# Padded value weights filled by quarters of a tile's tokens, a second projection half kept through a layer, and thirteen row slots instead of fourteen

## What is computed

```
h = rmsnorm(x); proj = h @ w_in            # q, k, v, output gate, pool input, 8 gate columns
mix = concat(mLSTM heads, pooling group) @ w_out;  x = x + mix
q = rmsnorm(x) @ peer_wq                   # 8 heads x 2 halves of 128
top 16 of 128 keys per half, 16 best of the 256 sums -> 16 experts per head, 128 per token
x = x + sum over the 128 experts of gate * gelu(xn . u_tab[e]) * v_tab[e]
x = x + sigmoid(x @ w_gate) * (p[l] @ w_ple)
```

## Time and profile before

| | |
|---|---|
| median of 3 runs | 1910.49 us (1908.98 to 1910.65) |
| the profiled execution | 1893.48 us, its span 1891.7 us |
| TensorE, VectorE, ScalarE, GpSimd busy | 1079.0, 978.1, 192.3, 998.2 us |
| bytes moved | 685.11 MB, mean 362 GB/s |
| of these gathered rows | 553.72 MB in 1056 gathers |
| of these weight halves | 103 loads into `wring`, 2 into `kept`, 1 into `scratch`, 1 MB each |

### The profile page before, as it was taken

How to read it: one execution, slowest core, us unless ns; L and a number is a source line. 1 busy time by engine, 2 the same in 40 slices (tenths; PEclk the granted TensorE clock), 3 DMA queues, 4 the chain that set the end, 5 groups by cost and what they waited for, 6 DMA issues and landing times. The chain is left out here.

```text
span 1891.7 us, 17959 instructions
## 1 busy us (share of the span) xinstructions
PE 1079.0 (57%) x6318; PEld 499.7 (26%) x6318; DVE 978.1 (52%) x2585; ACT 192.3 (10%) x332; POOL 998.2 (53%) x1062
## 2 busy tenths in 40 slices
PE   8840257788955835385655874048885522045556
PEld 4420133433412422241112432024341211031113
DVE  1498975523445788954004576951344497850001
ACT  3200021201101200000000212000110000000002
POOL 0156534345465555656666353755446566656663
PEclk9965668789987967697676886578896765576678
DMA  8699869889999999989999799979999999999995
GB/s 333 244 359 379 337 244 410 337 359 399 357 360 406 423 410 421 404 343 419 371 366 386 256 421 365 408 286 418 368 337 366 402 374 381 396 330 372 368 367 206
DMA packets 172759, 685.11 MB, mean 362 GB/s; under 512 B 19616, under 2 KB 21344, under 8 KB 158190
## 3 DMA queue, kind: packets, MB, share of 16 engines
q0 software_dynamic: 152064, 553.72, 75.9%
q1 hardware_dynamic: 20606, 130.25, 17.3%
HBM read 677.66 MB, written 6.59 MB: 362 GB/s over the span
## 5 line engine op out<-in xcount | busy, mean ns | idle before, releaser
L2105 DVE SCALAR_TENSOR_TENSOR rows<-rows,acc 128x1024 f32<-128x1024 f32 x512 | 594.2, 1217 | 49.6 <-issue 26.7
L908 PE MATMUL bank<-wring,turned 128*128 128x512 f32 (+1 forms) x808 | 394.0, 635 | 40.6 <-DMA wring<-in_w 24.3
L1235 PE MATMUL acc<-rows,wz 128*32 128x512 f32 x1952 | 323.1, 783 | 143.6 <-DMA rows<-in_v,index_tb 102.6
L1450 POOL DMA_INDIRECT rows<-in_u,index_A x256 | 240.3, 939 | 303.2 <-DVE rows L2105 123.8
L1450 POOL DMA_INDIRECT rows<-in_v,index_ta x256 | 242.5, 947 | 234.1 <-PE acc L1235 142.2
L1450 POOL DMA_INDIRECT rows<-in_u,index_B x256 | 240.7, 940 | 179.1 <-DVE rows L2105 110.7
L1450 POOL DMA_INDIRECT rows<-in_v,index_tb x256 | 241.1, 942 | 138.7 <-issue 68.1
L908 PEld LDWEIGHTS bank<-wring,turned 128*128 128x128 f32 x808 | 160.5, 207 | 236.7 <-issue 205.7
L1235 PEld LDWEIGHTS acc<-rows,wz 128*32 128x32 f32 x1952 | 69.6, 130 | 351.9 <-issue 347.0
L1185 PE MATMUL bank<-xn_s,consts 128*128 128x128 f32 x256 | 48.6, 334 | 154.3 <-issue 154.3
L1185 PEld LDWEIGHTS bank<-xn_s,consts 128*128 128x128 f32 x256 | 42.9, 243 | 159.9 <-issue 159.9
(11 more groups left out here) (320 smaller groups left out, 1054.4 us busy)
## 6 DMA issues: line engine op xcount, KB each, us to landing
wring<-in_w SPq DMA_DIRECT2D x103, 1024.0 KB
out_sample<-scratch SPq DMA_DIRECT2D x2, 2128.5 KB
scratch<-in_c_s SPq DMA_DIRECT2D x2, 2064.0 KB
rows<-in_u,index_A POOLq DMA_INDIRECT x256
rows<-in_v,index_ta POOLq DMA_INDIRECT x256
rows<-in_u,index_B POOLq DMA_INDIRECT x256
rows<-in_v,index_tb POOLq DMA_INDIRECT x256
kept<-in_w SPq DMA_DIRECT2D x2, 1024.0 KB
```

The costliest lines, as they stand in the source:

```text
L908: ins = pe.matmul(ps[:, part], turned["A"][:, 4 * h + c, :], w[:, c, part], start=first, stop=end, skip_group_check=True)
L1235: ins = pe.matmul(acc[i * QUAD:(i + 1) * QUAD, c, :], wz[:, i, at:at + QUAD], row, start=first, stop=end, skip_group_check=True)
L1450: pool.indirect_dma_start(out=rows[:, n % RING, :], out_offset=None, in_=a[table], in_offset=bass.IndirectOffsetOnAxis(ap=which[:, at:at + ...
L2105: dve.scalar_tensor_tensor(u, u, 1.0, acc[:, :, :], ALU.mult, ALU.mult, accum_out=dots[kind][:, s:s + 1]).then_inc(u_used, 1)
```

## The change

`TURN` becomes 8: `wz` holds the weights of 8 tokens of each quad, `w_later` those of the other 24, and there is a refill in front of groups 8, 16 and 24 of each big tile. `KEPT` = 2 halves of the input projection are kept through a layer: the first halves of blocks 0 and 1, each with semaphores of its own. `RING` becomes 13. In bytes of a partition: `wz` 8704 to 4608, `w_later` 256 to 384, `rows` 57344 to 53248, `kept` 8192 to 16384.

```diff
-RING = 14
+RING = 13
-TURN = QUAD // 2
+TURN = QUAD // 4
+KEPT = 2
 def is_kept(e):
-    return e[0] == "project" and e[2:4] == (0, 0)
+    return e[0] == "project" and e[2] < KEPT and e[3] == 0
@@ groups_of
-            if KIND[t] != "S" and g == TURN:
-                out.append(("refill", t))
+            if KIND[t] != "S" and g and g % TURN == 0:
+                out.append(("refill", t, g // TURN))
@@ build
-        kept = sb("kept", P, 4, BLOCK)
+        kept = sb("kept", P, KEPT, 4, BLOCK)
-        wz = sb("wz", P, 4, TURN * (QUAD + 1) + TURN)
-        w_later = sb("w_later", P, 4, TURN)
+        wz = sb("wz", P, 4, TURN * (QUAD + 1) + QUAD - TURN)
+        w_later = sb("w_later", P, 4, QUAD - TURN)
-            return (QUAD + 1) * (g % TURN) + TURN - lane
+            return (QUAD + 1) * (g % TURN) + QUAD - TURN - lane
@@ TensorE
-                    pe.wait_ge(kept_in, 16 * (layer_of(PASS_TILES[e[1]][0]) + 1))
-                    return kept
+                    pe.wait_ge(kept_in[e[2]], 16 * (layer_of(PASS_TILES[e[1]][0]) + 1))
+                    return kept[:, e[2]]
-                        ins.then_inc(kept_used, 1)
+                        ins.then_inc(kept_used[j], 1)
-                if kind != "S" and g == TURN:
-                    pe.wait_ge(refilled, count(("refill",), ("refill", t)))
+                if kind != "S" and g and g % TURN == 0:
+                    pe.wait_ge(refilled, count(("refill",), ("refill", t, g // TURN)))
@@ SyncE
-            def load_kept(layer):
-                sp.dma_start(kept[:, :, :].rearrange("p c n -> p (c n)"), a["w"][layer, IN0]).then_inc(kept_in, 16)
-
-            load_kept(0)
+            def load_kept(layer, j):
+                sp.dma_start(kept[:, j].rearrange("p c n -> p (c n)"), a["w"][layer, IN0 + 2 * j]).then_inc(kept_in[j], 16)
+
+            for j in range(KEPT):
+                load_kept(0, j)
             for e in HALVES_IN_ORDER[0:WRING]:
                 load_half(e)
                 if e == HALVES_IN_ORDER[1]:
                     load_small()
-                    sp.wait_ge(kept_used, 2)
-                    load_kept(1)
+                    sp.wait_ge(kept_used[e[2]], 2)
+                    load_kept(1, e[2])
@@ VectorE
-                halves = ps[:, 0:P].rearrange("p (j n r) -> p j n r", j=4, n=2)
-                dve.tensor_copy(by_token(), halves[:, :, 0, :])
-                free(dve.tensor_copy(w_later[:, :, :], halves[:, :, 1, :]), "turn_w", t)
-
-            def refill(t):
-
-                dve.wait_ge(v_used, V_BY[PLACE["v", t, TURN * GROUP - 1]] // GROUP)
-                after(dve.tensor_copy(by_token(), w_later[:, :, :]), refilled)
+                turned_w = ps[:, 0:P].rearrange("p (j r) -> p j r", j=4)
+                dve.tensor_copy(by_token(), turned_w[:, :, 0:TURN])
+                free(dve.tensor_copy(w_later[:, :, :], turned_w[:, :, TURN:]), "turn_w", t)
+
+            def refill(t, n):
+
+                dve.wait_ge(v_used, V_BY[PLACE["v", t, n * TURN * GROUP - 1]] // GROUP)
+                after(dve.tensor_copy(by_token(), w_later[:, :, (n - 1) * TURN:n * TURN]), refilled)
```

More of the change, by code:

```diff
@@ L791, in build @@
         bank_free = [sem(f"bank_free{i}") for i in range(BANKS)]
-        kept_in, kept_used = sem("kept_in"), sem("kept_used")
+        kept_in, kept_used = [sem("kept_in_%d" % j) for j in range(KEPT)], [sem("kept_used_%d" % j) for j in range(KEPT)]
         half_used, u_used, v_used = sem("half_used"), sem("u_used"), sem("v_used")
@@ L2124, in by_token @@
             def by_token():
-                placed = wz[:, :, TURN:].rearrange("p j (r c) -> p j r c", c=QUAD + 1)[:, :, :, 0:1]
+                placed = wz[:, :, QUAD - TURN:].rearrange("p j (r c) -> p j r c", c=QUAD + 1)[:, :, :, 0:1]
                 return placed.rearrange("p j r o -> p j (r o)")
```

## The result

The changed kernel takes 1938.15 us (median of 4 runs, 1935.82 to 1941.39); the kernel before took 1909.74 us beside it (4 runs, 1902.11 to 1910.65). The ratio is 1.0152 [1.0108, 1.0196]: 28.4 us slower, where the prediction had 14.3 and a range up to 1934. The direction and the largest mechanism were right; the size was not.

What follows compares the result with a forecast made beforehand. A stream of gathers feeds the kernel, held in turn by TensorE, DMA, VectorE and GpSimd's issue. Terms 2.4 - 2.2 - 2.5 + 3 + 13.6 = +14.3 us gave 1924.8 us, range 1905 to 1934.

Steps and rivals of the forecast that it cites:

- Thirteen slots: One row less ahead after consumer hold-ups costs one gather issue in gather-bound stretches: +3 us, bounds 0 to 6.2.
- five phases that end in a gather-bound stretch: Dots and values of tile 1, dots of tiles 3 and 4, values of tile 4: 0 to 1.24 us each.
- the next term: The refills' term, said to cover the values of tiles 0 and 3: +13.6 us.
- The start: Second kept half loads ahead of small loads, so gate matmuls wait for `m_s`: +2.4 us, bounds 0 to 3.0.
- The refills: Before group 24 of tiles 0 and 3, TensorE waits for VectorE's copy behind `choose`: +6.6 and +7.0, together +13.6 us.
- The second kept half: Fewer loads: -2.5 us for passes 2 and 3 together, -2.2 us in pass 1.
- The ring wait near 297 us: TensorE's 2.2 us wait in pass 1 for a half of block 2 vanishes, as it loads earlier: -2.2 us.
- The sum: Whole kernel: all terms together +14.3 us, 1924.8 us as a median, 0.75% slower.
- Rival A: Planner puts group 23 and its refill before the first `best`, the 13.6 us fall away: 1911 us; chance 0.22.
- rival B: Only one of tiles 0 and 3 is hit, or both by half: +7.7 us, 1918; chance 0.20.
- rival C: DMA traffic is the real bound, slot costs nothing, refills come early: -4.8 us, 1905.7; chance 0.20.

Runs made afterwards that it cites:

- f4: Kernel before with thirteen slots on the chip, planner still counting fourteen, so order of work unchanged: 1743.83 us beside 1734.01, 1.0061.
- h2: Repeat of thirteen slots with the kernel before's own schedule, timed against the kernel before: 0.70% slower.
- f1: The changed kernel run again, unaltered, against the kernel before: 1752.36 us beside 1734.01, 1.0107.
- h1: The changed kernel repeated beside its parts, against the kernel before: 1.0117.
- k1: The changed kernel repeated beside its version with one kept half, against the kernel before: 1.0101.
- e4: Changed kernel with groups 23 and 24 and the refill between them moved ahead of both `best` in tiles 0 and 3: 1761.72 us, 1.016 against the kernel before.
- e3: Changed kernel with SyncE's first loads in order of need, small loads before the second ring half: 1747.52 us, 1.0068 against the kernel before.
- after: The changed kernel with the whole change, first timed against the kernel before: 1938.15 us for 1909.74, 1.0152.
- e2: Kernel before with quarters and three refills only, one kept half and fourteen slots: 1744.18 us, 1.0057.
- g3: Quarters, one kept half and a fifteenth slot, against the kernel before: 1919.82 us beside 1908.27, 1.0053.
- g4: Quarters, one kept half, fifteen slots, last refill between the two `best`, group 25 ahead of `soften`: 1925.34 us beside the kernel before's 1908.27, 1.0077.
- g1: Changed kernel with one kept half (`KEPT = 1`), against the kernel before: 1950.34 us beside 1908.27, 1.0206.
- h4: Changed kernel with one kept half, repeated on the faster kind of chip, against the kernel before: 1.0115.
- k2: Changed kernel with one kept half, repeated beside the changed kernel, against the kernel before: 1.0114.
- the first comparison: The changed kernel's first timing beside the kernel before, 4 runs each: 1938.15 us for 1909.74, 1.0152.
- f3: Changed kernel with first loads in order of need and the refill before group 24 between the two `best`: 1744.78 us beside the kernel before's 1734.01, 1.0071.
- f2: The kernel before, unchanged, 8 runs for a profile beside the others on the same chip: 0.9993.
- h3: Repeat of quarters and three refills alone, fourteen slots, one kept half, against the kernel before: 0.91% slower.

## Why the prediction was wrong, point by point

**Thirteen slots: the failed step.** The prediction said "I count five phases that end in a gather-bound stretch [...] half: +3 us". Measured with an unchanged order of work: 0.61% and 0.70%, 9.8 and 12.4 us, above even its upper bound of 6.2. Two things were wrong in it. First, it left stretches out. The dots of tile 0 weren't counted, and the values of tiles 0 and 3 were said to be "in the next term", which then priced only the refill there. By VectorE's dots in f4 and h2 these stretches cost 4.4 and 4.6 us, nearly all in tile 0. Second, the five phases that it did count, with the sample tiles between them, cost 5.1 and 5.3 us and not 3, and the dots of tile 3 alone 2.0, where 1.24 was the most for a phase. Group 10 of tile 0 shows how a slot is lost: TensorE alternates between bursts of other matmuls and groups, and the slots are what it catches up with after each burst. There one slot less cost 1.92 us.

**The start: right place, too small.** The wait for `m_s` is 2.64 us (2.14 in f1, 1.85 in h1, 2.49 in k1, 1.27 in e4) where 2.4 was forecast. Missed was what TensorE does after it: 5.38 to 6.72 us for the first ring half in these five instead of some 3.6, at a granted clock of 0.50 in h1's slice of 18 to 22 us, the lower of the two levels, after an idle of 1.85 us. Before and in e3, without the wait, the clock stays at 1.00. The first gather went out at 90.67 to 91.60 us in the five profiles that have both kept halves in front (after, f1, h1, k1, e4; mean 91.2), at 85.47 to 88.04 in the twelve with one (mean 86.8), and at 84.85 to 88.03 in the three with e3's order (mean 86.0). So the start costs 4.4 us, 2.0 more than forecast. Where the first kept half lands moves too, between 7.5 and 10.2 us, but in kernels of either kind, so it isn't the change.

**The refills: right.** Order, place and waiting gather came as derived, and the size nearly so. Forecast 13.6 us; alone they cost 0.57% and 0.91%, 10.3 and 16.4 us, and the gathers of e2 lose 8.0 and 8.6 us at the two places. In after, where GpSimd comes late to them anyhow, each stall is 6.8 to 7.2 us instead of 9.3, and the gathers lose 5.2 to 5.3 and 5.9 to 6.0 us there (f1, h1, k1). On the faster kind of chip the other six refills added cost nothing that the runs can tell from these; g3 and g4 leave it open for the slower kind.

**The second kept half: its gain fits the forecast, but is spent by its own start.** Forecast -4.7 us beside the start. On the faster kind of chip after and after with one kept half are level: 1.0117 and 1.0115, 1.0101 and 1.0114, a mean of 0.05% or 1 us in favour of two, with intervals of 0.2% (3.5 us) on each. With 4.4 us lost at the start, it brings some 5 us elsewhere, give or take as much as the intervals. The ring wait near 297 us, which was to vanish, is gone in after; g1, with one kept half, still has 1.21 us of it at 301.96. On the faster kind of chip it isn't there with one kept half either (h4, k2), so that part of the term can't be told there.

**The sum.** On the faster kind of chip: 4.4 (start) + 11 (slot) + 13 (refills) - 5 (kept half) = 23 us. Measured were 18.4, 20.9 and 15.5. The parts aren't quite additive, since a gather that is late already waits less at the next stall: the refills' two places cost 11.2 us by the gathers in after and 16.6 in e2. With the slot at 11 and the start at 4.4 the prediction's own sum would have been +24.3 us.

**What stays open.** In the first comparison the loss was 28.4 us, on a chip where the kernel before takes 1910 and not 1733 us; and there after stood at 1.0152 while the same kernel with one kept half stood at 1.0206 (g1, in another set of runs). This suggests that on such a chip a kept half is worth more (0.5%, some 10 us, net of its start). The two never ran side by side there, and their intervals overlap, so it is not shown. Nor was the slot, the start or the refills timed alone on such a chip, so the 4 us between 24.3 and 28.4 are unexplained. Rival A (refills early) and rival B (one tile only) are excluded by the profile of after, and rival C (faster) by the time. A's price was wrong too: in e4 and f3 a refill placed earlier moves the wait on.

No version tried beats the kernel before. The best form of the whole change has e3's start, at 1.0068.

## What to carry to other kernels

Price a buffer slot over every stretch, also those that another term of the sum deals with, and over every place where its consumer works in bursts; a run with one slot less and the order of work unchanged measures it in one go. A copy of 0.2 us on an in-order engine costs what stands in front of it on that engine, and moving it up only pays if the one that it waits for is done by then: ask at each candidate place which wait comes next. And keep resident loads behind what the first matmuls need, since a short wait of TensorE can be paid twice, by the wait and by the slower clock after it.

## What the runs showed of the hardware

The same program took 1733 us on some chips and 1909 on others. One difference shows in GpSimd's gathers. With 16 of them in a pure value stretch, the fast kind needs 19.9 us, 1.24 each, the slow kind 22.8: there GpSimd stands for some 3.3 us once in 16 gathers, and no engine of the kernel ends that idle time. The kernel before on the first chip, GpSimd in that stretch, and its row in the waits of the whole span:

```profile
920.75 0.94 POOL L1450 DMA_INDIRECT rows<-in_v,index_tb  x1 [3.25 <-remote]
```
```profile
POOL rows L1450 <- remote: 51.2, 25, 3.3
```

After has 59.5 us of this in 35 waits on that chip; f1 and f2 have none. What causes it wasn't tried. The 51.2 us are less than a third of the 176 us between the two kinds. A second difference is TensorE's longest wait for a weight half: 18.61 us in the kernel before on the first chip, 1.7 in f2. The rest wasn't looked into.

TensorE's granted clock fell from 1.00 to 0.50 after an idle of 1.85 us at 15.65 us (h1), and was 1.00 again in the slice of 26 to 30 us. An idle alone doesn't do it: in h3 TensorE was idle for 2.95 us up to 9.97 us, and the clock was 1.00 in each slice of 4 us from 10 to 26 us.
